# Moving most of the next tile's projections and its gated linear attention into the indexer scoring loop

## What is computed

```python
def hybrid_mixer(h, w_in, w_gla_a2, b_gla_a, g_gla_norm, w_out):
    proj = h @ w_in            # h = rmsnorm(x), 2904 columns
    (aq, ak, av, iq, ik, iw, gq, gk, gv, ga, gg) = jnp.split(proj, offsets, axis=-1)
    ...
    o_attn = dsa_attention(aq, ak, av, iq, ik, iw)
    log_a = jax.nn.log_sigmoid(ga @ w_gla_a2 + b_gla_a) / GLA_TAU
    o_gla = gla(gq, gk, gv, log_a, gg, g_gla_norm)
    return jnp.concatenate([o_attn, o_gla], axis=-1) @ w_out

# dsa_attention, for a block of 128 queries:
    logits = einsum('bthd,bsd->bths', iqb, ik) * IDX_DIM ** -0.5
    score = einsum('bths,bth->bts', relu(logits), iwb)     # then causal mask
    _, idx = lax.top_k(score, 256)                         # attend to these keys only
```

## Time and profile before

| | |
|---|---|
| median of 6 runs | 18,724.68 us (18,710.33 to 18,806.47) |
| the profiled execution | 18,639.83 us, span of its slowest core 18,638.5 us |
| spans of the cores | 18,485.2 to 18,638.5 us |
| busy in the span | PE 64%, DVE 51%, ACT 29%, POOL 5% |
| chain that ended last | PE 42%, DVE 37%, issue 8%, DMA 6%, ACT 4%, POOL 2% |
| largest line of that chain | DVE L720 (counting passes), 23% |

### The profile page before, as it was taken

How to read it: one execution, slowest core, us unless ns; L and a number is a source line. 1 busy time by engine, 2 the same in 40 slices (tenths; PEclk the granted TensorE clock), 3 DMA queues, 4 the chain that set the end, 5 groups by cost and what they waited for, 6 DMA issues and landing times.

```text
span 18638.5 us, 217724 instructions; the slowest of 8 cores (18485.2 to 18638.5 us)
## 1 busy us (share of the span) xinstructions
PE 11965.2 (64%) x69376; PEld 6211.5 (33%) x69376; DVE 9577.4 (51%) x11480; ACT 5353.5 (29%) x11011; POOL 956.3 (5%) x1458
## 2 busy tenths in 40 slices
PE   5888864455555556555666665665665757388888
PEld 3666642222222222222222222222222222166666
DVE  1111213445555666666666766776777777222222
ACT  1111112223232333333333333343343434211111
POOL 1111110000000000000000000000000000011111
PEclk9888876667777777777777777787787878699999
DMA  3000010000000000000000000000000000200000
GB/s 57 28 28 28 28 35 16 14 14 11 11 11 11 8 10 7 8 10 7 7 7 7 4 7 7 7 4 7 7 4 7 4 7 4 48 28 28 33 28 28
DMA packets 106995, 293.29 MB, mean 16 GB/s; under 512 B 14608, under 2 KB 14880, under 8 KB 105888
## 3 DMA queue, kind: packets, MB, share of 16 engines
q1 hardware_dynamic: 86784, 236.70, 3.7%
q0 software_dynamic: 19104, 42.66, 1.5%
HBM read 221.31 MB, written 100.66 MB: 17 GB/s over the span
## 4 chain that ended last, share of the span: by engine, by line
PE 42%; DVE 37%; issue 8%; DMA 6%; ACT 4%; POOL 2%; DVEq 1%; ACTq 0%; POOLq 0%; SPq 0%
DVE mxcj L720 23%; PE ffn1pgu L243 7%; PE ffn2pgu L243 7%; PE mxpb L695 5%; PE mxpb L464 4%; PE mxpb L676 4%; PE ffn1pd L260 4%; PE ffn2pd L260 4%; DVE mxR L692 2%; PE mxacc L794 2%; DMA mxxt<-x_scr 2%; ACT mxR L689 2%; DVE mxbs L704 2%; DVE mxbs L702 2%; DMA x_scr<-mxxt 1%
## 5 line engine op out<-in xcount | busy, mean ns | idle before, releaser
L720 DVE TENSOR_SCALAR_CACHE_REDUCE mxcj<-mxsc,mxmid 128x384 uint8<-128x384 f32 (+61 forms) x992 | 4637.5, 4675 | 87.9 <-DVE mxmid L727 3.5
L766 ACT ACTIVATE mxPT<-mxpb 128x512 bf16<-128x512 f32 x4160 | 2261.8, 595 | 847.9 <-PE mxacc L768 678.2
L695 PE MATMUL mxpb<-mxR,mxWsel 128*128 128x512 bf16 (+3 forms) x4352 | 1693.3, 393 | 592.5 <-ACT mxR L689 295.2
L692 DVE TENSOR_SCALAR mxR<-mxpb 128x512 bf16<-128x512 f32 (+3 forms) x2176 | 1446.8, 665 | 700.0 <-PE mxpb L676 651.0
L689 ACT ACTIVATE mxR<-mxpb 128x512 bf16<-128x512 f32 (+3 forms) x2176 | 1208.0, 577 | 1704.0 <-PE mxpb L676 1387.7
L755 PE MATMUL mxpb<-mxI,mxMB 128*128 128x512 bf16 x4160 | 1613.0, 388 | 53.0 <-DVE mxMB L739 53.0
L752 PE MATMUL mxpb<-mxQT,mxKT 128*128 128x512 bf16 x4160 | 1611.1, 387 | 8.3 <-DVE mxsc L698 8.3
L676 PE MATMUL mxpb<-mxcmb,mxIQT 128*128 128x512 bf16 (+3 forms) x4352 | 1555.7, 400 | 0.0
L768 PE MATMUL mxacc<-mxPT,mxVaug 128*65 128x512 bf16 x4160 | 1419.4, 385 | 68.1 <-ACT mxPT L766 33.9
L779 PE MATMUL mxpb<-mxxt,mxones 1*64 1x512 f32 x256 | 205.8, 897 | 1561.8 <-ACT mxxt L778 1556.7
L485 PE MATMUL mxptr<-c_idb,mxxs 128*128 128x128 bf16 x512 | 64.7, 306 | 1668.4 <-DVE mxxs L482 1668.4
(11 more groups left out here) (171 smaller groups left out, 14409.2 us busy)
## 6 DMA issues: line engine op xcount, KB each, us to landing
ffn1xin<-x SPq DMA_DIRECT2D x64, 512.0 KB, 4.1
x_scr<-ffn1xin SPq DMA_DIRECT2D x64, 512.0 KB, 2.9
mxxt<-x_scr SPq DMA_DIRECT2D x64, 512.0 KB, 3.2
mxxt<-x_scr SPq DMA_DIRECT2D x128, 256.0 KB, 2.6
x_scr<-mxxt SPq DMA_DIRECT2D x128, 256.0 KB, 2.0
ffn2xin<-x_scr SPq DMA_DIRECT2D x64, 512.0 KB, 3.8
out<-ffn2xin SPq DMA_DIRECT2D x64, 512.0 KB, 2.6
mxwin<-w_in POOLq DMA_DIRECT2D x16, 363.0 KB, 4.4
```

The lines of the kernel that those rows point to most:

```text
L692: S.op(S.dve, lambda e: e.tensor_scalar(out=R[r][:, 0:wdt], in0=lb[:, 0:wdt], scalar1=0.0, scalar2=None, op0=ALU.max), reads=[lbb], writes ...
L695: S.op(S.pe, lambda e: e.matmul(sb_[:, 0:wdt], lhsT=Wsel[:, j, :], rhs=R[r][:, 0:wdt], start=(j == 0), stop=(j == 7)), reads=[b_R[r], b_Ws ...
L720: S.op(S.dve, lambda e: e.tensor_scalar(out=cj[:, 0:NK], in0=sc[:, 0:NK], scalar1=mid[:, 0:1], scalar2=None, op0=ALU.is_ge, op1=ALU.add, a ...
L766: S.op(S.act, lambda e: e.activation(out=PT[r][:], in_=pb_[:, :], func=AF.Exp, scale=0.125), reads=[pbb], writes=[b_PT[r]])
```

## The change

A and B are split in two. The "late" part of A is the projections of AQ and IQ; the "late" part of B is the transposes of the gated output. The rest of both, the "main" part, is issued inside `tile_C`: one piece of tile i+1 behind each weighting matmul of tile i. There are 16 pieces, so the first two blocks of keys take them all; what is left of them is issued behind the loop. The main parts get PSUM banks of their own: pool 4 and the two halves of `acc` for A, pool 4 alone for B. The scores of all blocks now go to pool 3. The chain that `bisect` takes from is shorter, and `SCHED` issues it from pass 11 on. In the diff the new indentation of unchanged lines is not shown.

```diff
@@ -304,5 +304,5 @@
 NIN = 2904
 NIT = 16
-SCHED = {10: 1, 11: 2, 12: 3, 13: 4, 14: 5, 15: 6}
+SCHED = {11: 1, 12: 2, 13: 2, 14: 2, 15: 3}
 BIG = 240000.0
 IWS = (8.0 ** -0.5) * (64.0 ** -0.5)
@@ -409,8 +409,18 @@
 
         def rot(key, lo, n):
+            if key == "a":
+                bl = bankset[0]
+                k = rc[key] % len(bl)
+                rc[key] += 1
+                return bl[k]
             k = lo + rc[key] % n
             rc[key] += 1
             return pool[k], b_pool[k]
 
+        banks_all = [(pool[k], b_pool[k]) for k in range(5)]
+        banks_A = [(pool[4], b_pool[4]), (acc[:, 0:512], b_acc[0]), (acc[:, 512:1024], b_acc[1])]
+        banks_B = [(pool[4], b_pool[4])]
+        bankset = [banks_all]
+
         win_v = W["w_in"].rearrange("(kc p) n -> p kc n", p=128)
         hw = NIN // 2
@@ -473,7 +483,9 @@
                      reads=[b_win, b_hT], writes=[bb])
 
-        def tile_A(i):
+        def tile_A(i, part, banks):
             r0 = i * 128
+            bankset[0] = banks
             QT, b_QT = QTs[i % 2], b_QTs[i % 2]
+            if part == 'main':
             S.dma(S.sp, xt[:], xi[r0:r0 + 128, :], reads=[xi_b[i]], writes=[b_xt])
             S.op(S.act, lambda e: e.activation(out=xs[:], in_=xt[:], func=AF.Square, accum_out=st[:, 0:1]),
@@ -488,4 +500,5 @@
                                                   in1=gcol[:].unsqueeze(2).to_broadcast([128, KC, 128]),
                                                   op=ALU.mult), reads=[b_ptr, b_c], writes=[b_hT])
+            if part == 'late':
             yield
             bk, bb = rot("a", 0, 5)
@@ -559,6 +573,8 @@
             return acc[:, a * 512 + f * 128:a * 512 + (f + 1) * 128]
 
-        def tile_B(i):
+        def tile_B(i, part, banks):
+            bankset[0] = banks
             ogT, b_ogT = ogTs[i % 2], b_ogTs[i % 2]
+            if part == 'main':
             bk, bb = rot("a", 0, 5)
             S.op(S.pe, lambda e: e.matmul(bk[:, 0:256], lhsT=gaT[:], rhs=wa2[:], start=True, stop=True),
@@ -653,5 +670,5 @@
             S.op(S.act, lambda e: e.copy(out=ogT[:], in_=ptr[:, 0:4, :]), reads=[b_ptr], writes=[b_ogT])
 
-        def tile_C(i):
+        def tile_C(i, g1):
             NK = 128 * (i + 1)
             S.op(S.dve, lambda e: e.tensor_tensor(out=L[:], in0=iwtok[:].unsqueeze(2).to_broadcast([128, 8, 16]),
@@ -670,5 +687,5 @@
                 wdt = min(512, NK - kb * 512)
                 kts = [b_IKT[t] for t in range(kb * 4, kb * 4 + wdt // 128)]
-                sb_, sbb = pool[3 + kb % 2], b_pool[3 + kb % 2]
+                sb_, sbb = pool[3], b_pool[3]
 
                 def LG(j):
@@ -696,6 +713,10 @@
                                                   start=(j == 0), stop=(j == 7)),
                          reads=[b_R[r], b_Wsel], writes=[sbb])
+                    next(g1, None)
                 S.op(S.dve, lambda e: e.tensor_copy(out=sc[:, kb * 512:kb * 512 + wdt], in_=sb_[:, 0:wdt]),
                      reads=[sbb], writes=[b_sc])
+            for _ in g1:
+                pass
+            bankset[0] = banks_all
             bis = NK > TOPK
             if bis:
@@ -822,13 +843,19 @@
                 yield from g_
 
-        run_all(tile_A(0))
-        run_all(tile_B(0))
+        run_all(tile_A(0, 'main', banks_all))
+        run_all(tile_A(0, 'late', banks_all))
+        run_all(tile_B(0, 'main', banks_all))
+        run_all(tile_B(0, 'late', banks_all))
         for i in range(NT):
-            tile_C(i)
+            if i + 1 < NT:
+                g1 = chain([tile_A(i + 1, 'main', banks_A), tile_B(i + 1, 'main', banks_B)])
+            else:
+                g1 = iter(())
+            tile_C(i, g1)
             parts = []
             if i >= 1:
                 parts += [tile_D(i - 1), tile_E(i - 1)]
             if i + 1 < NT:
-                parts += [tile_A(i + 1), tile_B(i + 1)]
+                parts += [tile_A(i + 1, 'late', banks_all), tile_B(i + 1, 'late', banks_all)]
             g = chain(parts)
             if 128 * (i + 1) > TOPK:
```

More of the change, by code:

```diff
@@ L649, in tile_B @@
-            yield
-            for h in range(4):
-                S.op(S.pe, lambda e: e.transpose(ptr[:, h, :], ogla[:, h, :], C.idb[:]),
-                     reads=[b_ogla, C.b], writes=[b_ptr])
-            S.op(S.act, lambda e: e.copy(out=ogT[:], in_=ptr[:, 0:4, :]), reads=[b_ptr], writes=[b_ogT])
-        def tile_C(i):
+                    rows = slice(a * 64, (a + 1) * 64)
+                    ab, abb = rot("a", 0, 5)
+                    S.op(S.pe, lambda e: e.matmul(ab[:, 0:128], lhsT=kin[rows, f, :], rhs=qd[rows, f, :],
+                                                  start=True, stop=True), reads=[b_kin, b_qd], writes=[abb])
@@ new lines, in tile_B @@
+                    S.op(S.dve, lambda e: e.tensor_tensor(out=AT[h % 2][:], in0=ab[:, 0:128], in1=TriU[:], op=ALU.mult),
+                         reads=[abb, b_c], writes=[b_AT[h % 2]])
+                    o_ = oreg(h)
+                    S.op(S.pe, lambda e: e.matmul(o_, lhsT=AT[h % 2][:], rhs=gvbf[:, h * 128:(h + 1) * 128],
+                                                  start=True, stop=False),
+                         reads=[b_AT[h % 2], b_gv], writes=[b_acc[a]])
+                    S.op(S.pe, lambda e: e.matmul(o_[0:64, :], lhsT=qd[rows, f, 0:64], rhs=S0[rows, f, :],
+                                                  start=False, stop=True),
+                         reads=[b_qd, b_S0], writes=[b_acc[a]])
@@ new lines, in tile_B @@
+                    S.op(S.pe, lambda e: e.matmul(o_[64:128, :], lhsT=qd[rows, f, 64:128], rhs=S1[rows, f, :],
+                                                  start=False, stop=True),
+                         reads=[b_qd, b_S1], writes=[b_acc[a]])
+                yield
+                state_step(1, S0, b_S0)
+                yield
+                for h in range(4):
+                    S.op(S.act, lambda e: e.activation(out=junkg[:], in_=oreg(h), func=AF.Square,
+                                                       accum_out=st[:, 4 + h:5 + h]),
+                         reads=[b_acc[h % 2]], writes=[b_junkg, b_stg])
@@ new lines, in tile_B @@
+                rstd_ops(S, C, st[:, 4:8], st[:, 8:12], st[:, 12:16], 4, 1.0, b_stg, b_stg, dim=128)
+                yield
+                for h in range(4):
+                    S.op(S.dve, lambda e: e.scalar_tensor_tensor(out=ogla[:, h, :], in0=oreg(h),
+                                                                 scalar=st[:, 12 + h:13 + h],
+                                                                 in1=ggs[:, h * 128:(h + 1) * 128],
+                                                                 op0=ALU.mult, op1=ALU.mult),
+                         reads=[b_acc[h % 2], b_stg, b_gg], writes=[b_ogla])
@@ L656, in tile_C @@
+            if part == 'late':
+                yield
+                for h in range(4):
+                    S.op(S.pe, lambda e: e.transpose(ptr[:, h, :], ogla[:, h, :], C.idb[:]),
+                         reads=[b_ogla, C.b], writes=[b_ptr])
+                S.op(S.act, lambda e: e.copy(out=ogT[:], in_=ptr[:, 0:4, :]), reads=[b_ptr], writes=[b_ogT])
+        def tile_C(i, g1):
             NK = 128 * (i + 1)
```

275 lines of the change are left out of this document (126 added, 149 removed).

## The result

| | before | after |
|---|---|---|
| median | 18,715.6 us (20 runs) | 18,983.8 us (10 runs, 18,901.1 to 19,121.5) |
| ratio to before | | 1.0155, 95% interval 1.0122 to 1.0187 |
| the profiled execution | 18,639.8 us | 18,927.3 us |
| up to the first tile's scoring (L657, now L674) | 2,867.3 us | 2,898.8 us |
| from there to the last mask | 13,094.0 us | 13,338.8 us |

The ratio compares the fast runs of both kernels, so it isn't the quotient of the two medians. The last two rows are means over the tiles with index 2 to 62: from L657 (L674) to the first maximum, and from there to the mask. So the passes with their tail gave 38.4 us a tile and the scoring stage took 42.4. The difference over 61 tiles is 248 us; the other three tiles take 3 back, and the mixer is 245 us longer.

The account below looks back on a forecast made before the run. VectorE's own queue was taken to set the tail's end, its waits for A and B counting in full. 2,659 us added, less 28, less 2,480, is 151; 18,640 + 151 + 85 = 18,875 us, range 18,470 to 19,200.

Parts of the forecast that it names:

- the sum: Whole kernel: 63 tiles at 42.2 us, less 28 for one-block tiles, less 2,480 from the tail: 151 us slower.
- The tail: Counting passes: all VectorE work of A and B leaves, with its waits, saving 2,480 us, 39.4 us a tile.
- What stays there: Tail: AQ and IQ matmuls, transposes and input load stay hidden, costing nothing new; uncovered, 8 us a tile and 3.6 us.
- The stretch: First two scoring blocks: pieces and steps add up in a row, 16.2 us becoming 52.0 at full clock, some 58 in profile.
- The clock: Scoring loop: half clock from the end of piece 6 raises the added 35.8 us a tile to 42.2.
- 47 us throughout: Rival, scoring loop: half clock from piece 3 on, 47 us a tile, 453 us slower, 19,180 us; chance 0.13.
- The single bank: Changes of scoring block: waiting for the score copy taken as zero; one more 0.1 us wait would be 48 us.
- The four tiles with one block: Scoring loop: eight steps fewer, some 0.9 us each, so 28 us less in all.
- The clock held: Rival, scoring loop: waits leave the clock up, 35.8 us a tile, 240 us faster, 18,485 us; chance 0.17.
- The steps did not fit into the gaps: Rival, scoring loop: steps run in the pieces' waits, 24.3 us a tile, 17,775 us, half of it some 18,300; chance 0.10.
- The tail's waits: Rival, tail: VectorE waits for AQ and IQ or the load instead, +1,240 us, some 20,100; chance 0.04.
- the bank did not stall: Rival, block changes: single score bank stalls 0.5 us at 480 changes, +240 us, 19,115 us; chance 0.04.

Follow-up runs that it names:

- behind: The changed kernel with all sixteen pieces issued behind the scoring loop, ahead of the first maximum, nothing interleaved: ratio to before 0.9898, 18,610 us.
- warm: The changed kernel with needless transposes on TensorE where it waits inside B, to keep it active: ratio to before 0.9992 (0.9887 to 1.0097).
- one_bank: The kernel before with the scores of every block in pool 3, nothing else changed: ratio to before 0.9986 (0.9939 to 1.0032).
- fine_tail: The changed kernel with 34 cut pieces, spread, ahead of the weighting matmul, and the tail cut likewise from pass index 8: 17,078 us, ratio to before 0.9024.
- fine_dense: The changed kernel with 34 pieces cut at every wait, one per step from the first, ahead of the weighting matmul: ratio to before 0.9425.
- fine_after: The changed kernel with 34 pieces cut at every wait, spread evenly over the steps, behind the weighting matmul: ratio to before 0.9532.

## Why the prediction was right, point by point

The forecast was 18,875 us, 0.8% slower, and the direction, the mechanism and the size of both sides hold. The net loss is a small difference of two large terms: 245 us in the mixer, where the sum had 151.

- **The tail.** Forecast 39.4 us a tile, measured 38.4. The rows of A and B did leave it; the passes behind them wait 17 us more in sum and take 11 us more beside that, as their records overlap less with those before them. 1.0 us a tile is 61 of the 94 us between 245 and 151; the rest of the 61 was not taken apart.
- **What stays there** costs nothing, as said: L826 and L833 wait as before, the load of the next input is hidden (L494 idle 27 us, where L482 had 502), and the 128 matmuls stand behind E's.
- **The stretch.** "Some 58 us": 56.8. By the sum's own terms it was 56.6 (52.0, 3.0 for L573 and the heads, 1.6 for the projections); the 1.8 us of the third block lie behind it and came as 1.7. The working inside was off in two places that cancel, so that the length came out is in part luck. The pieces were priced at 40.5 of the 52.0 us at full clock and the steps at 11.5; behind shows 35.9 for the pieces alone, the clock's fall included, which leaves 20.9 of the 56.8 for the steps between them. That "they add up in a row" was too mild: 4.5 us of overlap are lost besides.
- **The clock.** Forecast 6.4 us a tile (42.2 less 35.8); warm gave back 3.8, net of what its own transposes cost. The half clock at the heads and in the third block came; but the projections behind the second piece ran at full clock in the tile shown, and the four matmuls of L573 (now L589) took 1.06 us in the median tile and 0.60 in the 11 fastest of 63, the one shown among them: 0.46 more at half clock, where the sum had 0.51. The Trainium skill, "TensorE: Matmul & The Clock Gate", section "HAM oscillation — how this bites in real kernels", had the direction right: the granted clock fell from 1.00 to 0.50 behind TensorE's wait of 4.22 us for the logarithms. 47 us throughout, as it would have given, did not come.
- **The single bank.** Taken as zero, with 48 us for "one more wait of 0.1 us": it is that wait which came, 0.11 us at each change of block, 41 to 53 us in the kernel before. The hand-over from the copy is 0.15 us, as in the sum; the term set at nothing is the second wait. At the two changes of block among the pieces the sum had the copy in its row; the sign named for the bank, idle time that ends with the copy, is the 252.7 us of L712.
- **The four tiles with one block** were to be 28 us cheaper, 7 each. Those with index 2 and 3 lose 42.3 us (9.5 to 51.8) and 40.1, nearly like the others; the first two have no passes and were not taken apart. Over the 61 tiles the scoring stage lost 27 us more than the forecast had for them. With the tail's 61 us this makes 88 of the 94.
- **The rivals.** The clock held only where work was added to hold it. The steps did not fit into the gaps, for the reason given, the order of the queues: one line of order was worth 10.7 us a tile, and cutting the pieces 10.3 more. The tail's waits did not come back (L826 and L833), and the bank did not stall in the kernel before. Of interleaving the Trainium skill, "Perfetto Trace Analysis", section "Optimization Strategy", says that it may help; here it lost 6.0 us a tile against none as the change has it, and gained 16.1 with the pieces cut (85.7 to 91.7 and to 69.6). What the list of rivals lacked is the kernel without interleaving: by the sum's own terms (40.5 us a tile for the pieces, 39.4 out of the tail) no gain, in fact 1.0%.

## What to carry to other kernels

Before a chain of work is put into a pipelined loop, read the order that each in-order queue will get: an instruction that waits for another engine stops all that the loop has behind it, and a loop that runs ahead of itself may lose that too. Cut the chain at every wait, issue a step's own work first, and the consumer a step behind its producer; how widely the pieces are spread matters little then. And price the version with no interleaving: it shows what the overlap itself is worth.

## What the runs showed of the hardware

The feed-forward network ahead of the mixer, the same code in all these kernels, took from 2,741 to 3,068 us up to the first tile's scoring, and the granted clock goes with it. Its first 2,700 us in one_bank and in fine_tail:

```profile
0.00:2700.00 2700.00, 2011.13 (x14592) 1452.59 (x14592) 494.94 (x901) 407.19 (x963) 327.68 (x510) 0.91 0.15 36
```

```profile
0.00:2700.00 2700.00, 2219.03 (x13664) 1494.37 (x13665) 462.97 (x841) 386.98 (x899) 275.57 (x417) 0.79 0.12 31
```

That is more than the whole effect of the change. The two ran on different chips, but on one chip it was 2,748 us at 0.91 in fine_dense and 2,980 at 0.83 in fine_after, and in the one execution of the change the eight cores lie between 2,734 and 2,899. The mean clock of a span doesn't show it, since the mixer is half of waits; two profiled executions of this kernel are compared by stage, and totals only by repeated runs.

A wait can cost time though what it waits for is long there. The first weighting matmul of a block starts 0.145 us after its rectification with one wait in TensorE's queue, and 0.250 us after it with a second one, for a copy that had ended before (385 changes of block each, in the kernel before and in one_bank).
